# The column order of float32r products in a three-layer kernel on one core

## The reference

```python
def squared_relu_mlp(h, w_up, w_down):
    u = jax.nn.relu(h @ w_up)
    return (u * u) @ w_down

def first_block(x, ...):
    for layer in range(DEPTH):
        mix = hgrn2_mixer(...) if layer < N_A else diff_attn_mixer(...)
        h = h + rms_norm(mix, ...)
        ff = squared_relu_mlp(rms_norm(h, mlp_norm_pre[layer]), mlp_w_up[layer], mlp_w_down[layer])
        h = h + rms_norm(ff, mlp_norm_post[layer])

def second_block(x, ...):
    z = rmsnorm(x, mix_pre_norm[i]) @ w_in[i]
    a = mla(...)                                     # w_uq, w_ukv, causal attention
    c = short_gated_conv(...)
    x = x + rmsnorm(m @ w_out[i], mix_post_norm[i])
    f = (jax.nn.silu(h @ w_gate[i]) * (h @ w_up[i])) @ w_down[i]
    x = x + rmsnorm(f, ffn_post_norm[i])
    x = x + jax.nn.sigmoid(x @ w_ple_gate[i]) * e    # e from p @ w_ple_proj
```

## Time and profile before

| What | Value |
|---|---|
| runs | 964.62, 965.25, 965.69 us; median 965.25 |
| span of the profiled execution, first to last instruction | 963.2 us |
| TensorE busy; loads of weights | 952.3 us (99%), 7530 records; 909.1 us (94%) |
| DVE busy | 748.2 us (78%) |
| ACT busy | 547.7 us (57%) |
| POOL busy | 89.4 us (9%) |
| DMA queue of the weights | 163.47 MB, 55.5% of the 16 engines' span |
| mean rate of all DMA | 173 GB/s |

### The profile page before, as it was taken

The page is one execution under the profiler, slowest core; times in us unless marked ns, Lnnn a source line. Parts: engine busy times, 40 slices in busy tenths (PEclk is TensorE's granted clock), DMA queues, the critical chain, the costliest instruction groups (busy, mean ns, idle before and its releaser), DMA issues.

```text
span 963.2 us, 18430 instructions
## 1 busy us (share of the span) xinstructions
PE 952.3 (99%) x7530; PEld 909.1 (94%) x7530; DVE 748.2 (78%) x1129; ACT 547.7 (57%) x819; POOL 89.4 (9%) x91
## 2 busy tenths in 40 slices
PE   9999999999999999999999999999999999999998
PEld 8999999999999998999999999999999999999998
DVE  6998778978855599867987844489887998787777
ACT  6652366656454476756665544455666665556455
POOL 5334101000201000001000201001001000000000
PEclk9999999999999999999999999999999999999999
DMA  8733444766666836436476575626636467665651
GB/s 256 243 120 115 143 128 140 218 200 197 195 183 193 267 109 197 150 113 183 136 215 197 176 214 184 194 68 182 183 110 202 127 197 214 187 190 170 203 175 44
DMA packets 164723, 166.62 MB, mean 173 GB/s; under 512 B 6784, under 2 KB 162832, under 8 KB 164640
## 3 DMA queue, kind: packets, MB, share of 16 engines
q1 hardware_dynamic: 162752, 163.47, 55.5%
q0 software_dynamic: 1056, 1.19, 0.5%
q10 hardware_dynamic: 832, 0.79, 0.4%
HBM read 163.82 MB, written 1.08 MB: 171 GB/s over the span
## 4 chain that ended last, share of the span: by engine, by line
PE 82%; DVE 12%; issue 2%; ACT 2%; DMA 2%; SPq 0%; POOL 0%; ACTq 0%; DVEq 0%
PE ps L657 19%; PE ps L660 16%; PE ps L649 13%; DVE w_lo L1990 4%; PE ps L676 3%; PE ps L677 3%; PE ps L678 3%; PE ps L682 2%; PE ps L683 2%; PE ps L684 2%; PE ps L689 2%; PE ps L609 2%; PE ps L617 2%; PE ps L690 2%; PE ps L691 2%
## 5 line engine op out<-in xcount | busy, mean ns | idle before, releaser
L1990 DVE TENSOR_TENSOR w_lo<-w_raw,w_hi 128x1024 fp32r<-128x1024 f32 (+4 forms) x314 | 375.0, 1205 | 116.1 <-ACT w_hi L1424 110.3
L1424 ACT ACTIVATE w_hi<-w_raw 128x1024 fp32r<-128x1024 f32 x298 | 313.3, 1056 | 200.3 <-PE ps L660 47.6
L657 PE MATMUL ps<-xs,w_hi 128*128 128x256 f32 x1012 | 132.6, 277 | 0.0
L657 PEld LDWEIGHTS ps<-xs,w_hi 128*128 128x128 f32 x1012 | 127.0, 188 | 4.5
L660 PE MATMUL ps<-xs,w_lo 128*128 128x256 f32 x832 | 112.2, 277 | 0.0
L660 PEld LDWEIGHTS ps<-xs,w_lo 128*128 128x128 f32 x832 | 102.9, 188 | 0.2
L682 PE MATMUL ps<-xs,w_hi 128*128 128x256 f32 x320 | 91.4, 285 | 0.4 <-DVE w_lo L1990 0.4
L683 PE MATMUL ps<-xs,w_hi 128*128 128x256 f32 x320 | 89.3, 279 | 0.0
L684 PE MATMUL ps<-xs,w_lo 128*128 128x256 f32 x320 | 89.3, 279 | 0.0
L649 PE MATMUL ps<-xs,w_hi 128*128 128x512 f32 x326 | 85.1, 393 | 0.3 <-DVE mo L2018 0.2
L1431 ACT ACTIVATE tmp<-ps 128x512 f32<-128x512 f32 x75 | 44.5, 593 | 70.6 <-PE ps L649 62.6
(11 more groups left out here) (431 smaller groups left out, 1896.6 us busy)
## 6 DMA issues: line engine op xcount, KB each, us to landing
w_raw<-in_mlp_w_up SPq DMA_DIRECT2D x64, 512.0 KB, 4.2
w_raw<-in_mlp_w_down SPq DMA_DIRECT2D x64, 512.0 KB, 3.5
w_raw<-in_a_w_in SPq DMA_DIRECT2D x32, 512.0 KB, 4.3
w_raw<-in_w_gate SPq DMA_DIRECT2D x22, 512.0 KB, 3.8
w_raw<-in_w_up SPq DMA_DIRECT2D x22, 512.0 KB, 4.6
w_raw<-in_w_down SPq DMA_DIRECT2D x20, 512.0 KB, 4.4
w_raw<-in_w_kv SPq DMA_DIRECT2D x16, 512.0 KB, 4.3
w_raw<-in_w_in SPq DMA_DIRECT2D x16, 512.0 KB, 3.9
```

What stands on the lines that cost most here:

```text
L657: mm(ps[:, 2 * pset + n, at], hi[:, kk, n * P:(n + 1) * P], x[:, kt0 + kk, at], start=False, stop=False)
L1424: o = fn(dst, raw, ACT.Copy)
L1990: return v.tensor_tensor(d, x, y, ALU.subtract)
```

## The change

In every float32r product the columns of the moving operand, and those of the output in `ps`, are taken in another order. `in_turns` splits the columns into two halves, and each half into blocks of 16, and lists them so: the last block of the first half, the last block of the second half, the block ahead of it in the first half, the one in the second half, and so on to the first block. In a product of 256 columns a half is 128 columns, 512 bytes in a partition, and there are 16 blocks; in one of 512, a half is 256 columns, 1024 bytes, and there are 32. Since input and output have the same order, each result lands where it landed before. The weights are read as before. No product is added or dropped, and their order, waits and semaphores stay. Float32 matmuls are not changed.

All products are issued from the helper `prod` now, so a profile of the changed kernel has them all on one line.

```diff
+TURN = 16
...
+            def in_turns(ap):
+                return ap.rearrange("p (k l e) -> p l k e", k=2, e=TURN)[:, ::-1]
+            def prod(o_ap, w, x, start, stop):
+                return mm(in_turns(o_ap), w, in_turns(x), start=start, stop=stop)
...
-                    mm(o_ap, hi[:, w], x[:, kt, 0:S], start=kt == 0 and (kind == "feat" or n == 0), stop=False)
-                    mm(o_ap, lo[:, w], x[:, kt, 0:S], start=False, stop=False)
+                    prod(o_ap, hi[:, w], x[:, kt, 0:S], start=kt == 0 and (kind == "feat" or n == 0), stop=False)
+                    prod(o_ap, lo[:, w], x[:, kt, 0:S], start=False, stop=False)
...
-                            o = mm(ps[:, 2 * pset + n, :], hi[:, kk, n * P:(n + 1) * P], x[:, kt0 + kk, :],
+                            o = prod(ps[:, 2 * pset + n, :], hi[:, kk, n * P:(n + 1) * P], x[:, kt0 + kk, :],
...
-                            mm(ps[:, bank, 0:S], hi[:, kk, w], x[:, kt, 0:S], start=first, stop=False)
-                            mm(ps[:, bank, 0:S], hi[:, kk, w], x[:, kt, S:2 * S], start=False, stop=False)
-                            o = mm(ps[:, bank, 0:S], lo[:, kk, w], x[:, kt, 0:S], start=False, stop=last)
+                            prod(ps[:, bank, 0:S], hi[:, kk, w], x[:, kt, 0:S], start=first, stop=False)
+                            prod(ps[:, bank, 0:S], hi[:, kk, w], x[:, kt, S:2 * S], start=False, stop=False)
+                            o = prod(ps[:, bank, 0:S], lo[:, kk, w], x[:, kt, 0:S], start=False, stop=last)
...
```

More of the change, by code:

```diff
@@ L616, in low_records @@
                     o_ap = ps[:, 2 * pset + n, S:2 * S] if kind == "feat" else ps[:, pset, n * S:(n + 1) * S]
-                    o = mm(o_ap, hi[:, n * P:(n + 1) * P], x[:, kt, S:2 * S], start=False,
+                    o = prod(o_ap, hi[:, n * P:(n + 1) * P], x[:, kt, S:2 * S], start=False,
                            stop=kt == KT - 1 and (kind == "feat" or n == 1))
@@ L681, in quantum @@
                             at = slice(n * S, (n + 1) * S)
-                            mm(ps[:, pset, at], hi[:, kk, w], x[:, kt, 0:S], start=first and n == 0, stop=False)
-                            mm(ps[:, pset, at], hi[:, kk, w], x[:, kt, S:2 * S], start=False, stop=False)
-                            o = mm(ps[:, pset, at], lo[:, kk, w], x[:, kt, 0:S], start=False, stop=last and n == 1)
+                            prod(ps[:, pset, at], hi[:, kk, w], x[:, kt, 0:S], start=first and n == 0, stop=False)
+                            prod(ps[:, pset, at], hi[:, kk, w], x[:, kt, S:2 * S], start=False, stop=False)
+                            o = prod(ps[:, pset, at], lo[:, kk, w], x[:, kt, 0:S], start=False, stop=last and n == 1)
                         elif kind == "one_bank_tok":
@@ L688, in quantum @@
                             at = slice(n * S, (n + 1) * S)
-                            mm(ps[:, pset, at], xh, hi[:, kk, :], start=first and n == 0, stop=False)
-                            mm(ps[:, pset, at], xh, lo[:, kk, :], start=False, stop=False)
-                            o = mm(ps[:, pset, at], xl, hi[:, kk, :], start=False, stop=last and n == 1)
+                            prod(ps[:, pset, at], xh, hi[:, kk, :], start=first and n == 0, stop=False)
+                            prod(ps[:, pset, at], xh, lo[:, kk, :], start=False, stop=False)
+                            o = prod(ps[:, pset, at], xl, hi[:, kk, :], start=False, stop=last and n == 1)
                         else:
@@ L694, in quantum @@
                             xl = x[:, kt, S + n * P:S + (n + 1) * P]
-                            mm(ps[:, bank, 0:S], xh, hi[:, kk, :], start=first, stop=False)
-                            mm(ps[:, bank, 0:S], xh, lo[:, kk, :], start=False, stop=False)
-                            o = mm(ps[:, bank, 0:S], xl, hi[:, kk, :], start=False, stop=last)
+                            prod(ps[:, bank, 0:S], xh, hi[:, kk, :], start=first, stop=False)
+                            prod(ps[:, bank, 0:S], xh, lo[:, kk, :], start=False, stop=False)
+                            o = prod(ps[:, bank, 0:S], xl, hi[:, kk, :], start=False, stop=last)
                 return o
@@ L1142, in short_tile @@
                 o_ap, xk = ps[:, bank, n * S:(n + 1) * S], xs_s[:, xi + kt, :]
-                mm(o_ap, w_hi[:, s, cols], xk[:, 0:S], start=first, stop=False)
-                mm(o_ap, w_hi[:, s, cols], xk[:, S:2 * S], start=False, stop=False)
-                return mm(o_ap, w_lo[:, s, cols], xk[:, 0:S], start=False, stop=last)
+                prod(o_ap, w_hi[:, s, cols], xk[:, 0:S], start=first, stop=False)
+                prod(o_ap, w_hi[:, s, cols], xk[:, S:2 * S], start=False, stop=False)
+                return prod(o_ap, w_lo[:, s, cols], xk[:, 0:S], start=False, stop=last)
             pe.wait_ge(xs_ready, XS0["cq"] + 1)
@@ L1269, in ple_tiles @@
                         xk = xs_s[:, 4 + kt, :]
-                        mm(o_ap, ple_hi[kt][:, cols], xk[:, 0:S], start=kt == 0 and n == 0, stop=False)
-                        mm(o_ap, ple_hi[kt][:, cols], xk[:, S:2 * S], start=False, stop=False)
-                        o = mm(o_ap, ple_lo[kt][:, cols], xk[:, 0:S], start=False, stop=kt == 1 and n == 1)
+                        prod(o_ap, ple_hi[kt][:, cols], xk[:, 0:S], start=kt == 0 and n == 0, stop=False)
+                        prod(o_ap, ple_hi[kt][:, cols], xk[:, S:2 * S], start=False, stop=False)
+                        o = prod(o_ap, ple_lo[kt][:, cols], xk[:, 0:S], start=False, stop=kt == 1 and n == 1)
                 if n == 1 and kt == 1:
```

16 lines of the change are left out of this document (8 added, 8 removed).

## The result

The changed kernel takes 974.95 us (974.79 to 975.24, four runs) against 965.47 for the kernel before in the same comparison: a ratio of 1.0097, with a 95% interval of 1.0083 to 1.0111. It is 9.5 us slower, where I had said 948 us and a range of 925 to 967.

The account below looks back on a forecast made before the run. Spacing of matmuls on TensorE was taken as the bound. Savings of 10.2 + 7.4 + 3.5 = 21.1 us, times 0.82, left 17.3, so 965.25 - 17.3 = 948 us; range 925 to 967.

Parts of the forecast that it names:

- What bounds the kernel: TensorE, 82% of the chain of waits: there the kernel is as long as its matmuls are far apart, start to start.
- Cost of the pieces: Broken or reversed column order in float32r products: taken as nothing, with 4 ns per product as the upper end.
- Saving of the order: Float32r products were to come closer together, down to the next bound behind the columns: 21.1 us in all.
- (a): 2,376 256-column products go from the long spacing (117.5 ns) to the short (113.2): 10.2 us, taken in full.
- (b): 6,162 256-column products go from the short spacing to 112 ns, 1.2 ns each: 7.4 us, taken in full.
- (c): 567 512-column products go from 228.3 to 216 ns: 7.0 us, of which half, 3.5, was taken.
- The floor: A 256-column product cannot fall much below 112 ns, since loading its weights sets the pace there (line 936).
- The factor of 0.82: TensorE's share of the chain: elsewhere shorter products only meet waits earlier, so 17.3 of 21.1 us are left.
- The first: Rival: the columns' order does not matter, every interval stays, 965 us; chance 0.13.
- The second: Rival: each jump to the other half costs, giving 994 us or 1014 us; chance 0.17.
- The sign that I had set for it: Intervals of 120 ns and more in the profile after would mean that the pieces have a price.

Follow-up runs that it names:

- write_only: Kernel before with only the output written in the new order, the moving operand read in plain order: 965.70 us (kernel before beside it: 966.83).
- turn64: Changed kernel with blocks of 64 columns in place of 16: 965.29 us (kernel before beside it: 966.75).
- plain_32w: Kernel before, plain order, with only the first 32 of 128 weight columns loaded in most feat products: 965.03 us (kernel before: 965.10).
- even_odd: Changed kernel with blocks of 16 in ascending order, first all even ones, then all odd ones: 998.09 us (kernel before beside it: 965.34).
- forward: Changed kernel with the same turns between the halves, but from first block to last: 997.36 us (kernel before beside it: 966.83).

## Why the prediction was wrong

**What bounds the kernel: right.** The intervals between matmuls decide. The products' intervals grew by 8.6 us, and the span by 9.8.

**Cost of the pieces: right on the writing side, unfounded on the other.** `write_only` shows no cost for broken or reversed writing, as lines 1071 and 917 had led me to say. The Trainium skill, "Advanced Engine Details and Errata", section "PSUM Cachelines", says that any non-contiguous pattern significantly slows matmuls, which spoke against the change; for writing in runs of sixteen this is not borne out: 115.2 ns with and without. But I let line 917, which reads in steps, speak for the reading of float32r products as well. Records of float32 matmuls take two ticks per column, and I had noted myself that they lose next to nothing at that pace (216 ns for 256 columns, line 826); a row of an operation that shows no such loss cannot bound what the order of reading costs one that does.

**Saving of the order: the step that failed.** I had it that the order of the columns is what the change alters, that the columns lose time at full pace, and concluded that the order would give some of it back. Nothing in the trace said in which direction. The three terms came out so: (a) long to short, 10.2 us expected, 2.9 gained, since the long spacing fell by 1.2 ns of 4.3; (b) from the short spacing to the floor of 112, 7.4 us gain expected, and 11.5 lost by the products that had the short spacing; (c) 512 columns, 3.5 gain expected, 0.1 or less either way. In none of the runs did another order or place do better than plain order with the activations 64 bytes off, and it held the short spacing in six products of ten. The change put one spacing in the place of two, nearer to the long one.

**The floor: not what holds these products.** I took the 112 ns of line 936, which I read as paced by its weights, as what a product would fall to. `plain_32w` shortens the load by 80 ns and leaves the interval at 113.8, so the load of weights is not what keeps it there, and that the two numbers lie close is no sign of a common cause. No kernel brought its products down to 112, so the bound itself was not tested.

**The factor of 0.82: wrong for a loss.** 8.6 us more in the intervals made 9.8 more in the span; nothing was taken up in waits, which grew by 1.6 us.

**The rivals.** The first, that the order does not matter, is refuted (965 to 998 us by order alone). The second had the sign but not the cause: there is no price per jump, by `turn64` and by four means for 16 pieces. The sign that I had set for it, intervals of 120 ns and more, did appear, in 1,182 of 6,061 products against 57 of 6,063 before, in turn with shorter ones; it does not tell a price per jump from another cause. Its 0.17 was too little. What should have raised it was in the earlier trace rows and in the code: that most products already sat at the short spacing and that 64 bytes of placing had been found worth having point to a tuned relation between the two operands, which a new order may give up; more products stood to lose 3 ns or more than to gain 4.

**What stays open.** Why the short spacing is 113.3 ns and not the 106.7 of bare ticks; by which rule an order and a phase come to 113, 116.6, 118.8 or 120 (parity of lines, lines out of sequence and length of the load each fail on one run or more); and what puts a stretch of plain products into the long spacing: it gets rarer with a load of 16 columns, and the direct products of `us` fell into it when only `xs` was moved. Weights read in the other direction, which would show whether the two directions matter against each other, were not tried.

## What to carry to other kernels

Before predicting what an access order does, ask which way the present one is off: if equal products show several spacings, find out which the most of them have and what each would move to, because one new order can move them all. Bound a price only by rows of operations that run at the same pace on the same resource. And where a kernel's placing of operands in SBUF is deliberate, treat order and placing as one thing, and measure both operands' sides.

## What the runs showed of the hardware

- The order in which a float32r product reads its moving columns is worth up to 5.1 ns in 115.2 (`even_odd`), and up to 10.5 ns in 229.5 for 512 columns (`forward`), with a mean granted clock of 0.999 or 1.0 in each run. The order of writing, in runs of sixteen columns, is worth nothing that shows (115.2 both ways).
- 64 bytes between the places of the moving and the standing operand are worth 4.4 ns in plain order (`xs` 115.4 to 119.8), and it shows as well where only the standing tile was moved (tok 116.4 to 119.7). The load of weights grows with it, from 188 to 191 or 192 ns. The Trainium skill, "TensorE: Matmul & The Clock Gate", section "Step-by-step: what each phase is for", says that loading the next tile's weights takes no SBUF read bandwidth from the running matmul. Shortening the load indeed changed little here (113.8 ns with a quarter of its columns, 114.0 before); where the two operands lie changed more, which that sentence does not lead one to expect.
- The records of weight loads last 188, 108 and 94 ns for 128, 32 and 16 columns: 0.83 ns per column and some 81 ns beside it.
